# Norm work moved to token classes over a five-unit tail of two projections in a hybrid transformer layer

## The reference, cut to what matters

```python
mix = (g_ssd * y_ssd + g_sc * y_sc) @ w_o
x = x + gt1 * rmsnorm(mix, mix_post_g)
h = rmsnorm(x, ffn_pre_g) * (1.0 + sc2) + sh2
u = causal_dwconv(h @ w_up, ffn_conv_w, ffn_conv_b)      # width 3 over tokens
u_gate, u_val = jnp.split(u, 2, axis=-1)
f = (jax.nn.silu(u_gate) * u_val) @ w_down
x = x + gt2 * rmsnorm(f, ffn_post_g)
...
h = rmsnorm(x, norm_w_2)                                 # second block, then h @ w_in_2
```

## Time and profile before

| | us |
|---|---|
| median of 3 runs | 1561.02 (1560.79 to 1561.41) |
| profiled execution, its own time | 1561.39 |
| span of that execution | 1559.6 |
| TensorE matmul busy | 1504.3 (96%) |
| GpSimd busy | 974.2 (62%) |
| VectorE busy | 800.7 (51%) |
| ScalarE busy | 542.0 (35%) |

### The profile page before, as it was taken

The page is one execution under the profiler, slowest core; times in us unless marked ns, Lnnn a source line. Parts: engine busy times, 40 slices in busy tenths (PEclk is TensorE's granted clock), DMA queues, the critical chain, the costliest instruction groups (busy, mean ns, idle before and its releaser), DMA issues.

```text
span 1559.6 us, 21459 instructions
## 1 busy us (share of the span) xinstructions
PE 1504.3 (96%) x7486; PEld 1229.7 (79%) x7486; DVE 800.7 (51%) x964; ACT 542.0 (35%) x859; POOL 974.2 (62%) x949
## 2 busy tenths in 40 slices
PE   3899999999999999999899999999899999999998
PEld 3688888888888888877688888888678888888876
DVE  5647666576566557331645555400373573836534
ACT  3353461362263121111522222200343645545432
POOL 1565666665765778676577777766557554545442
PEclk9899999999999999999899999999899999999999
DMA  8243433533533334224132222322342221111231
GB/s 334 83 132 106 142 122 129 162 113 110 186 108 113 105 133 162 95 82 149 57 105 94 94 94 94 107 96 95 104 164 94 68 68 68 67 67 67 74 116 54
DMA packets 65610, 172.08 MB, mean 110 GB/s; under 512 B 5616, under 2 KB 22128, under 8 KB 64912
## 3 DMA queue, kind: packets, MB, share of 16 engines
q1 hardware_dynamic: 45792, 151.47, 28.3%
q10 hardware_dynamic: 19760, 19.86, 4.0%
HBM read 167.05 MB, written 4.26 MB: 110 GB/s over the span
## 4 chain that ended last, share of the span: by engine, by line
PE 92%; DVE 4%; issue 1%; POOL 1%; DMA 1%; ACT 0%; SPq 0%; DVEq 0%; POOLq 0%
PE ps L501 17%; PE ps L504 17%; PE ps L503 17%; PE ps L518 6%; PE ps L520 6%; PE ps L519 6%; PE ps L792 3%; PE ps L793 3%; PE ps L794 3%; PE ps L940 2%; PE ps L966 2%; PE ps L952 1%; DVE acc L1539 1%; PE ps L689 1%; DVE xr L1890 1%
## 5 line engine op out<-in xcount | busy, mean ns | idle before, releaser
L468 POOL TENSOR_SCALAR w_hi<-raw 128x512 fp32r<-128x512 f32 x472 | 324.0, 705 | 560.4 <-PE ps L504 266.4
L473 POOL TENSOR_TENSOR w_lo<-raw,w_hi 128x512 fp32r<-128x512 f32 x472 | 655.3, 1410 | 0.0
L501 PE MATMUL ps<-h_hi,w_hi 128*128 128x512 f32 x984 | 390.2, 397 | 5.4 <-DVE h_lo L1565 4.2
L504 PE MATMUL ps<-h_hi,w_lo 128*128 128x512 f32 x984 | 384.1, 390 | 0.0
L503 PE MATMUL ps<-h_lo,w_hi 128*128 128x512 f32 x984 | 383.8, 390 | 0.0
L501 PEld LDWEIGHTS ps<-h_hi,w_hi 128*128 128x128 f32 x984 | 185.2, 188 | 49.2 <-issue 8.4
L504 PEld LDWEIGHTS ps<-h_hi,w_lo 128*128 128x128 f32 x984 | 185.1, 188 | 39.1
L503 PEld LDWEIGHTS ps<-h_lo,w_hi 128*128 128x128 f32 x984 | 185.4, 188 | 38.7 <-issue 1.4
L518 PE MATMUL ps<-h_hi,w_hi 128*128 128x512 f32 x368 | 148.4, 403 | 0.4 <-POOL w_lo L473 0.4
L520 PE MATMUL ps<-h_hi,w_lo 128*128 128x512 f32 x368 | 143.7, 390 | 0.0
L519 PE MATMUL ps<-h_lo,w_hi 128*128 128x512 f32 x368 | 143.4, 390 | 0.0
(11 more groups left out here) (259 smaller groups left out, 2332.6 us busy)
## 6 DMA issues: line engine op xcount, KB each, us to landing
raw<-stream SPq DMA_DIRECT2D x236, 512.0 KB, 3.2
ada_raw<-ada SPq DMA_DIRECT2D x64, 256.0 KB, 3.5
ada<-ada SPq DMA_DIRECT2D x16, 512.0 KB, 9.1
abc<-acs_dram ACTq DMA_DIRECT2D x16, 512.0 KB, 6.5
x_tok<-x SPq DMA_DIRECT2D x1, 2048.0 KB, 8.1
xr<-x_classes ACTq DMA_DIRECT2D x1, 2048.0 KB, 10.2
x_dram<-xr ACTq DMA_DIRECT2D x1, 2048.0 KB, 10.8
x_res<-x_dram ACTq DMA_DIRECT2D x2, 1024.0 KB, 7.7
```

The costliest lines, as they stand in the source:

```text
L468: ins = nc.gpsimd.tensor_scalar(w_hi[:, slot, w], raw[:, raw_slot, w], 1.0, 1.0, ALU.mult, ALU.mult).then_inc(split_hi, 1)
L473: ins = nc.gpsimd.tensor_tensor(w_lo[:, slot, w], raw[:, raw_slot, w], w_hi[:, slot, w].bitcast(F32), ALU.subtract)
L501: nc.tensor.matmul(ps[:, bank], w_hi[:, slot, w], x_hi[:, k0 + k], start=start and k == 0, stop=False)
L504: mm = nc.tensor.matmul(ps[:, bank], w_lo[:, slot, w], x_hi[:, k0 + k], start=False, stop=stop and k == tiles - 1)
```

## The change

The tail of each projection that runs class by class grows from two units to five (`OUTER`). All five units' weights are held at once: three in a new area (`wx_hi`, `wx_lo`), two in the usual slots. Class 0 runs over all five units, then class 1, then class 2; then class 0 is transposed, into its own two banks, and class 3 runs in two parts with the transposes of class 1 between. The norm's steps behind the transposes (`full`, `hi`, `lo`) go class by class over all features. `opening` is gone: the next stage's first two units run whole, one behind the other. Since banks no longer gather tokens in natural order, h now stands in class order after norm 1 too, and the feed-forward convolution adds tokens carried over from the preceding class by two more instructions a unit; `act_hi` and `act_lo` are then written without strided views.

```diff
-NORM_A, NORM_B = (0, 1, 2, 4), (3, 5, 6, 7)
+OUTER = 5
...
-        hn = at("hn", FREE + 104 * KB, [P, 4, S])
+        hn = at("hn", FREE + 96 * KB, [P, 2, D])
+        wx_hi = at("wx_hi", FREE + 72 * KB, [P, OUTER - 2, UW], F32R)
+        wx_lo = at("wx_lo", FREE + (72 + 4 * (OUTER - 2)) * KB, [P, OUTER - 2, UW], F32R)
...
+            def slot_and_users(u):
+                for end, dead in ((U_UP, U_WO), (U_ATT, U_DOWN + 12)):
+                    m = u - (end - OUTER)
+                    if 0 <= m < OUTER - 2:
+                        return 2 + m, dead
+                    if OUTER - 2 <= m < OUTER:
+                        before = [v for v in range(end - OUTER - 2, end - OUTER) if v % 2 == u % 2][0]
+                        return u % 2, before + 1
+                return u % 2, u - 1
...
             for u in range(2, UNITS):
-                pool.wait_ge(units_done, 1 + u - 1)
-                split(u, u % 4, u % 2, 16 * (u // 4 + 1))
+                slot, users = slot_and_users(u)
+                pool.wait_ge(units_done, 1 + users)
+                split(u, u % 4, slot, 16 * (u // 4 + 1))
...
+            def class_pass(r, u, operands, n, ms):
+                slots = outer_slots(u)
+                for m in ms:
+                    if r == 0:
+                        pe.wait_ge(split_done, u + m + 1)
+                    mm = one_class(r, slots[m], *operands[m], False, m == OUTER - 1)
+                    if r == NT - 1:
+                        mm.then_inc(units_done, 1)
+                    elif m == OUTER - 1:
+                        mm.then_inc(n["product"], 1)
+            def turn_rows(n, r):
+                pe.wait_ge(n["rows"], r + 1)
+                for b in range(DB):
+                    mm = nc.tensor.transpose(ps[:, 2 * r + b // 4, b % 4 * P:(b % 4 + 1) * P],
+                                             br[:, r, b * P:(b + 1) * P], ident)
+                mm.then_inc(n["turned"], 1)
+            def whole(u, bank, n):
+                pe.wait_ge(split_done, u + 1)
+                for k in range(KT):
+                    pe.wait_ge(n["lo"], 7 + k // 4)
...
+                mm.then_inc(units_done, 1)
+            def across_norm(n, u, operands, units, banks):
+                every = range(OUTER)
+                class_pass(0, u, operands, n, every)
+                class_pass(1, u, operands, n, every)
+                class_pass(2, u, operands, n, every)
+                turn_rows(n, 0)
+                class_pass(3, u, operands, n, range(3))
+                turn_rows(n, 1)
+                class_pass(3, u, operands, n, range(3, OUTER))
+                turn_rows(n, 2)
+                turn_rows(n, 3)
+                for u, bank in zip(units, banks):
+                    whole(u, bank, n)
...
+                def full(r):
+                    act.wait_ge(n["turned"], r + 1)
+                    if r >= 2:
+                        act.wait_ge(n["lo"], 2 * (r - 2) + 2)
+                    for b in range(4, DB):
+                        ins = A(hn[:, r % 2, b * P:(b + 1) * P], ps[:, 2 * r + 1, (b - 4) * P:(b - 3) * P],
+                                ACT.Identity, scale=scale(b), **shift(b))
+                    ins.then_inc(n["full_act"], 1)
+                def hi(r):
+                    for hv in range(2):
+                        act.wait_ge(n["full_act" if hv else "full_dve"], r + 1)
...
+                product(0, 0)
+                residual(0, 1)
+                product(1, 2)
+                residual(1, 3)
+                product(2, 4)
                 full(0)
                 hi(0)
+                residual(2, 5)
+                full(1)
+                hi(1)
+                product(3, 6)
+                full(2)
+                hi(2)
+                residual(3, 7)
+                full(3)
+                hi(3)
+                then()
...
+                residual(0, 0)
+                rows(0, 1)
+                residual(1, 2)
+                rows(1, 3)
+                residual(2, 4)
+                full(0)
+                lo(0)
+                rows(2, 5)
                 full(1)
+                lo(1)
+                residual(3, 6)
+                full(2)
+                lo(2)
+                rows(3, 7)
+                full(3)
+                lo(3)
...
+                        for k, late in ((1, 1), (0, 2)):
+                            if k == 0:
+                                dve.wait_ge(ffn_taps, 16 * i + 4 * j + 2)
+                            w = col("ffn_w", 16 * i + 4 * j + k)
+                            same, before = slice(late * P, S), slice(0, S - late * P)
+                            STT(fcv[:, j, same], ps[:, j, before], w, fcv[:, j, same], ALU.mult,
+                                ALU.add).then_inc(ffn_taps, 1)
+                            carried = fcv[:, j, 0:late * P].rearrange("p (r i) -> p r i", r=late)[:, :, 1:P]
+                            past = ps[:, j, S - late * P:S].rearrange("p (r i) -> p r i", r=late)[:, :, 0:P - 1]
+                            STT(carried, past, w, carried, ALU.mult, ALU.add).then_inc(ffn_taps, 1)
```

More of the change, by code:

```diff
@@ L311, in norm_sems @@
             return {n: sem(f"n{k}_{n}") for n in
-                    ("product", "squared", "root", "inverse", "scaled", "added", "rows", "rows_act", "turned",
+                    ("product", "squared", "root", "inverse", "scaled", "added", "rows", "turned",
                      "full_act", "full_dve", "hi", "lo")}
@@ L397, in halves, with weights, outer_slots @@
             return t.rearrange("p (h s) -> p h s", h=2)
+        def weights(slot):
+            if slot < 2:
+                return w_hi[:, slot], w_lo[:, slot]
+            return wx_hi[:, slot - 2], wx_lo[:, slot - 2]
+        def outer_slots(u):
+            return [2 + m for m in range(OUTER - 2)] + [(u + m) % 2 for m in (OUTER - 2, OUTER - 1)]
         def banks_of(r):
@@ L523, in tiles @@
                     mm.then_inc(signal, 1)
[L525 to L545, removed]
             pe.wait_ge(tab_in, 16)
@@ L789, in one_class @@
                 q = slice(r * P, (r + 1) * P)
+                hi, lo = weights(slot)
                 for hv in range(2):
                     out, w = ps[:, 2 * r + hv], slice(hv * S, (hv + 1) * S)
-                    nc.tensor.matmul(out, x_hi[:, q], w_hi[:, slot, w], start=first, stop=False)
-                    nc.tensor.matmul(out, x_hi[:, q], w_lo[:, slot, w], start=False, stop=False)
-                    mm = nc.tensor.matmul(out, x_lo[:, q], w_hi[:, slot, w], start=False, stop=last)
-                return mm
@@ L797, in last_by_class @@
[L797 to L804, removed]
+                    nc.tensor.matmul(out, x_hi[:, q], hi[:, w], start=first, stop=False)
+                    nc.tensor.matmul(out, x_hi[:, q], lo[:, w], start=False, stop=False)
@@ L808, in last_by_class @@
                         mm.then_inc(n["product"], 1)
[L810 to L821, removed]
@@ L824, in _ @@
-            for k in range(DB - 2):
+            def turn_rows(n, r):
[8 more added lines that the diff above has]
+                    pe.wait_ge(n["lo"], 7 + k // 4)
+                    w, slot = slice(k * P, (k + 1) * P), u % 2
+                    nc.tensor.matmul(ps[:, bank], w_hi[:, slot, w], h_hi[:, k], start=(k == 0), stop=False)
+                    nc.tensor.matmul(ps[:, bank], w_hi[:, slot, w], h_lo[:, k], start=False, stop=False)
+                    mm = nc.tensor.matmul(ps[:, bank], w_lo[:, slot, w], h_hi[:, k], start=False, stop=(k == KT - 1))
+                mm.then_inc(units_done, 1)
@@ L825, in _ @@
+            for k in range(DB - OUTER):
                 pe.wait_ge(mix_steps, 1 + 4 * (k + 1))
@@ L1908, in norm, with rows, full @@
[L1908 to L1914 removed]
+                def rows(r, k):
+                    inverse(k, 28, r)
+                    TS(br[:, r], xr[:, r], small[:, 28 + r:29 + r], None, ALU.mult).then_inc(n["rows"], 1)
+                def full(r):
+                    dve.wait_ge(n["turned"], r + 1)
+                    if r >= 2:
+                        dve.wait_ge(n["lo"], 2 * (r - 2) + 2)
+                    for b in range(4):
+                        ins = TS(hn[:, r % 2, b * P:(b + 1) * P], ps[:, 2 * r, b * P:(b + 1) * P], scale(b), shift(b),
+                                 ALU.mult, *((ALU.add,) if shift(b) is not None else ()))
+                    ins.then_inc(n["full_dve"], 1)
```

122 lines of the change are left out of this document (35 added, 87 removed).

## The result

The changed kernel takes **1582.97 us** (median of 4 executions, 1582.58 to 1584.07) where the kernel before takes 1561.22 (1560.79 to 1561.81) beside it: ratio **1.0139, 95% interval [1.0126, 1.0153]**. It is slower by 21.8 us; 19.6 were forecast. The profiled execution took 1582.58, with a span of 1580.8 and a mean granted clock of 0.983, against a span of 1559.6 before.

The account below looks back on a forecast made before the run. TensorE, 92% of the chain of waits, was taken as the bound. Norm 1 at 10.3 us slower and norm 2 at 9.3, nothing elsewhere, made 19.6 and a forecast of 1580.6 us; range 1568 to 1588.

Parts of the forecast that it names:

- Term 1: Pass 0 of the tail: GpSimd's weight splits come late, 6.5 us of new TensorE waits in norm 1.
- Term 5: Behind the tail: TensorE's clock falls to half while idle; turn(3) runs at half, the first whole-unit matmuls cost 1.9 us more.
- rival C: Tail's pass 0: the clock falls there too, 2 us more a norm, 1585 us; chance 0.12.
- Term 3: Norm's chain: ScalarE's and VectorE's in-order lists delay class 3; first whole unit starts 17.6 us behind its last matmul.
- Rival A: Norm's lists: they do not hold class 3 back, 5.6 us less a norm, 1569 us; chance 0.1.
- Term 2: Tail's passes 1 to 3: passes 1 and 2 take 6.8 us each; class 3 and two turns end at 35.4.
- term 4: Opening: no overlap with the norm, both units lie behind the last class, 10.9 us.
- Norm 2: Second norm, ahead of attention: same lists as norm 1, 9.3 us slower than before.
- Feed-forward loop: Convolution taps on VectorE: 1.9 us against 1.5 a unit, hidden by TensorE's matmuls, cost 0.
- Rival B: Tail's pass 0: GpSimd runs ahead, splits in time, 6.5 and 6.1 us less, 1568 us; chance 0.1.
- Rival D: Tail and norm: weights ahead and product(3) served at once, 3.7 us less a norm, 1554 us; chance 0.04.

Follow-up runs that it names:

- e2: Changed kernel with only the tail's passes 0 and 1 woven, each unit used for two classes before the next: 1578.03 us, ratio 1.0106 to the kernel before.
- e1: Changed kernel with only ScalarE's and VectorE's lists in the norm reordered, class 3's product ahead of hi(1): 1575.38 us, ratio 1.0086 to the kernel before.
- e4: Changed kernel with unread matmuls added, 46 ahead of turn(3) and 11 behind it: 1578.26 us, ratio 1.0104 to the kernel before.
- e7: Changed kernel with the opening in 256-column halves, woven first passes and partly reordered lists: 1562.99 us, ratio 1.0006 to the kernel before.
- e9: e7 with lists reordered again, turn(3) between the two units' first halves, and unread matmuls around turn(2): 1556.65 us, ratio 0.9966 to the kernel before.
- e10: e9 without the unread matmuls: 1558.24 us, ratio 0.9975 to the kernel before.
- e5: Kernel before with only h in class order and the changed feed-forward loop, four taps a unit: 1561.37 us, ratio 1.0000.
- e3: Changed kernel with both the reordered lists of e1 and the woven passes of e2: 1568.43 us, ratio 1.0042 to the kernel before.

## Why the prediction was right, point by point

The forecast was 10.3 + 9.3 us for the two norms and nothing elsewhere; measured were 11.22, 9.12 and nothing. The rows meant are those of the fences above.

- **Term 1, late weights: right.** From one matmul start to the next, past the usual 0.23, the third unit comes 717.74 - 715.67 - 0.23 = 1.84 late (1.9 forecast), the fourth and fifth 2.1 each (2.3). With the long first matmul behind each wait they make 6.4; 6.5 was forecast. GpSimd's pace held at 3.65 a split. e2 shows it by taking it away.
- **Term 5, the clock: one half missed.** The fall ahead of turn(3) came as forecast: turn(3) 1.97 us, and from `whole`'s first to the third w_up unit 12.53 (12.8 forecast). But the clock fell in pass 0 as well, which I had given 0.12 as rival C. The eight starts from 726.49 to 729.88 take 3.39 us and not 1.82: **1.6 us** that the sum for norm 1 lacks, more than its whole error of 0.92. Without it norm 1 would have come out at 9.6, 0.7 under the forecast, so part of the hit is that errors of opposite sign met. In norm 2 it fell one unit earlier (the matmul at 1108.71 lasts 0.79), and there it cost next to nothing: the slow matmuls filled time in which the fifth unit's weights were awaited (that wait is 0.70, not 2). So rival C's 2 us were nearly there in one norm and hidden in the other. That they were hidden is luck of this execution: in the traces of e1 and e4, with the same instructions up to the end of class 3, norm 2's tail took 2.1 and 2.2 us longer. Behind turn(3) the half clock cost 1.6 us and not 1.9 (12.53 against the 10.9 of 48 matmuls at full clock).
- **Term 3, queue order: right, in its parts too.** product(3) starts 3.05 us behind class 3's last matmul (38.9 - 35.4 = 3.5 forecast), and the square of class 3's x right behind hi(2). turn(2) waits 0.6 (1.2). From class 3's end to `whole` it is 767.48 - 750.30 = 17.2 us; 17.6 was forecast (53.1 - 35.4 makes 17.7). e1 proves it the other way round: with the lists changed, the square follows at once and 7.6 us come back. Rival A priced that at 5.6 a norm, too much: it is 3.8 and 3.5. Its sum made 12.1 us from class 3's end to `whole` (47.5 - 35.4); in e1, with the square held up by nothing, it is 764.59 - 751.19 = 13.4.
- **Term 2** held; **term 4** too, as an item of the sum: both whole units lie behind the last class, 12.53 us of them, 11.0 in e4 at full clock. It is no loss against before, where the opening took 12.85 us from its first matmul. e7, e9 and e10, which start half of it before class 3's rows are through, are the first to come level with before or under it, but their lists changed in the same edits. A slip in term 1's bound: five splits of 5.6 us would end pass 0 at 23, not 22.
- **Norm 2**: 9.12 against 9.3. `then()`'s transfers in their new place showed no wait on TensorE.
- **Feed-forward loop: right at 0.** VectorE's tap groups between 780 and 990:

```profile
L1956 DVE SCALAR_TENSOR_TENSOR fcv<-ps,tab,fcv 128x384 f32<-128x384 f32 x39 | 24.0, 615 | 56.9 <-ACT fcv L1352 56.9
L1956 DVE SCALAR_TENSOR_TENSOR fcv<-ps,tab,fcv 128x256 f32<-128x256 f32 x39 | 18.9, 484 | 5.4 <-DVE fcv L1960 1.4
L1960 DVE SCALAR_TENSOR_TENSOR fcv<-ps,tab,fcv 128x254 f32<-128x254 f32 x39 | 18.5, 473 | 0.0
...
L1960 DVE SCALAR_TENSOR_TENSOR fcv<-ps,tab,fcv 128x127 f32<-128x127 f32 x39 | 13.2, 339 | 0.0
```

  Together 615 + 484 + 473 + 339 ns = 1.91 us a unit, as estimated (1.9), in 5.44 of TensorE's. e5 agrees, within 1.6 us.
- **Rival B** (splits in time) fell with the waits for weights in the first timeline. **Rival D** (faster) needed weights in time and product(3) served at once. e3 has both and still lies 7.0 us over before, so D's route is not enough: the chain of class 3 and both opening units still stand in line behind the tail. Its clock "kept" had also no ground; e4 shows that this takes added work.

The Trainium skill, "GPSIMD Engine Reference", section 8, was cited for VectorE and GpSimd contending when VectorE has two SBUF inputs; the same sentence names its 2-port mode. e7's rows agree: the add and `lo`, with two SBUF inputs, slow down while GpSimd splits, and so does the 1024-column scale, whose mode no row names; the product step with an input in PSUM does not. The steps that slow down take 1.6 to 2.4 times as long.

## What to carry to other kernels

When work is cut into pieces so that engines overlap, the last piece's chain is what counts: lay the in-order lists out so that nothing of an earlier piece stands ahead of it, and see what of the next stage needs only the earlier pieces. Holding more operands at once makes their producer the bound for the first pass; weaving two passes took away 8.4 of 9.5 us of such waits, though alone most of that turned up in the next wait. Two fixes on one chain don't simply add up: what the weaving handed on to the waits for rows, the better lists caught in part, so measure them together. And a piece's chain that is no shorter than the whole's (17.2 us for one class, 15.5 for four) leaves nothing to win by cutting; look at that number first.

## What was not expected of the hardware

- The granted clock fell in pass 0 although TensorE worked 1.4 us between waits of about 2: 0.80 and 0.77 in two windows of norm 1, with matmuls 0.43 us apart (1.2 GHz) and 0.23 again behind them (2.4 GHz). With the passes woven, and one wait of some 0.7 us a norm left, it stayed at 1.00 in these windows. Where in the pass it fell was not fixed. In norm 1 it was behind the fifth unit in the changed kernel, at the fifth in e4, at the fourth in e1; in norm 2 at the fourth in the changed kernel, at the fifth in e1 and e4, which made that pass some 2 us longer.
- In e10 the clock came back in the midst of the 256-column matmuls, which follow every 0.21 us at half and 0.12 at full. In e4 and e9 it did not fall at all while unread matmuls ran.
- The 13.5 us of e4's unread matmuls in norm 1, on a bank that others had finished with, disturbed nobody that the rows show: VectorE's and ScalarE's share of the stretch stayed as it was (from 752 to 756 3.27 and 3.68 us busy, against 3.27 and 3.67 without).

What stays open: why the first w_o unit starts up to 2.7 us apart from trace to trace, which is more than some effects here; the claims above rest on medians and on stretches inside one trace, not on absolute starts. Open too is what the halves, the lists and the place of turn(3) each gave in e7, e9 and e10, and what the contention of VectorE and GpSimd costs there.
